# Constant products ahead of TensorE's long waits, the modulation sums over four layers, a reordered Fourier mixer

## The reference, cut to what matters

```
x = x + 0.5 * swiglu(rms_norm(x) ...)          # twice per layer, four times in block 1
u = rms_norm(x) @ w_in; x = x + concat(ssd(u), mlstm(u), rwkv7(u)) @ w_out
...
m = split(silu(c) @ ada_w[l] + ada_b[l])       # block 2, both for c and for c_ctx
h = rmsnorm(t) * (1 + m[scale]) + m[shift]
t = t + 0.5 * m[gate] * swiglu_2(h)            # before and after the mixer
layer 0: t = t + m[5] * (FFT2(h).real @ four_w + four_b)   # Fourier mixer
layer 1: retention mixer with rotary embedding, then a projection
return rmsnorm(x)
```

## Time and profile before

| | us |
|---|---|
| median of 3 executions | 3462.03 |
| lowest, highest | 3461.65, 3463.73 |
| the profiled execution's own time | 3463.73 |
| its span, first to last instruction | 3461.7 |
| PE busy in the span | 3247.6 (94%) |
| mean granted TensorE clock over the span | 0.972 |
| DVE, ACT, POOL busy | 2101.1 (61%), 1308.7 (38%), 115.8 (3%) |

### The profile page before, as it was taken

How to read it: one execution, slowest core, us unless ns; L and a number is a source line. 1 busy time by engine, 2 the same in 40 slices (tenths; PEclk the granted TensorE clock), 3 DMA queues, 4 the chain that set the end, 5 groups by cost and what they waited for, 6 DMA issues and landing times.

```text
span 3461.7 us, 45970 instructions
## 1 busy us (share of the span) xinstructions
PE 3247.6 (94%) x19010; PEld 2824.2 (82%) x19010; DVE 2101.1 (61%) x2545; ACT 1308.7 (38%) x1584; POOL 115.8 (3%) x126
## 2 busy tenths in 40 slices
PE   7998988999998898899999999999999999999998
PEld 7978877898988786798788877788878888787797
DVE  6757557776866657677775754775343333544654
ACT  4434244444435234543421233422233122444443
POOL 0001200000000210000000000000000000000000
PEclk9999999999999998999999999999999999999999
DMA  6542022555553112455443531343222222323452
GB/s 250 230 152 86 27 95 77 200 235 204 211 207 104 38 60 72 177 208 211 153 164 123 183 124 37 122 165 122 91 85 98 91 98 80 118 98 109 164 183 98
DMA packets 83835, 462.96 MB, mean 134 GB/s; under 512 B 7573, under 2 KB 11285, under 8 KB 43562
## 3 DMA queue, kind: packets, MB, share of 16 engines
q1 hardware_dynamic: 77952, 451.45, 35.6%
q10 hardware_dynamic: 5674, 8.57, 0.8%
HBM read 458.95 MB, written 1.05 MB: 133 GB/s over the span
## 4 chain that ended last, share of the span: by engine, by line
PE 64%; DVE 25%; ACT 7%; issue 2%; DMA 0%; ACTq 0%; POOL 0%; DVEq 0%; POOLq 0%
PE ps L100 64%; DVE lo L311 8%; DVE acc L459 5%; ACT hi L305 3%; PE ps L546 1%; DVE acc L456 0%; DVE m0restMs L1980 0%; DVEq L86 0%; DVE xt L701 0%; DVE f11rot L875 0%; DVE f10rot L875 0%; DVE f20rot L875 0%; ACT f20hf_h L853 0%; ACT f11hf_h L853 0%; ACT f10hf_h L853 0%
## 5 line engine op out<-in xcount | busy, mean ns | idle before, releaser
L311 DVE TENSOR_TENSOR lo<-raw,hi 128x2048 fp32r<-128x2048 f32 (+1 forms) x357 | 809.6, 2268 | 622.8 <-ACT hi L305 601.5
L305 ACT ACTIVATE hi<-raw 128x2048 fp32r<-128x2048 f32 (+1 forms) x357 | 676.1, 1894 | 572.7 <-PE ps L100 541.9
L459 DVE SCALAR_TENSOR_TENSOR acc<-raw,sil,acc 128x512 f32<-128x512 f32 x504 | 379.0, 752 | 20.7 <-DVE f21hf_l L877 0.5
L100 PE MATMUL ps<-half00hs,hi 128*128 128x512 f32 x672 | 209.3, 393 | 0.6 <-DVE lo L311 0.6
L100 PE MATMUL ps<-half02hs,hi 128*128 128x512 f32 x672 | 209.0, 392 | 0.7 <-DVE lo L311 0.7
L100 PE MATMUL ps<-half10hs,hi 128*128 128x512 f32 x672 | 208.7, 392 | 0.8 <-DVE lo L311 0.7
L100 PEld LDWEIGHTS ps<-half10hs,hi 128*128 128x128 f32 x672 | 125.7, 188 | 28.5 <-DVE lo L311 1.6
L100 PEld LDWEIGHTS ps<-half02hs,hi 128*128 128x128 f32 x672 | 125.4, 188 | 27.6 <-DVE lo L311 1.1
L100 PEld LDWEIGHTS ps<-half00hs,hi 128*128 128x128 f32 x672 | 125.2, 188 | 27.3 <-DVE lo L311 1.0
L100 PE MATMUL ps<-half10hs,lo 128*128 128x512 f32 x352 | 137.6, 391 | 0.0
L100 PE MATMUL ps<-half02hs,lo 128*128 128x512 f32 x352 | 137.6, 391 | 0.0
(11 more groups left out here) (919 smaller groups left out, 7900.3 us busy)
## 6 DMA issues: line engine op xcount, KB each, us to landing
raw<-in_ffn_w_gate_up SPq DMA_DIRECT2D x88, 1024.0 KB, 9.0
raw<-in_ffn_gu SPq DMA_DIRECT2D x88, 1024.0 KB, 5.0
raw<-in_ffn_w_down SPq DMA_DIRECT2D x85, 1024.0 KB, 5.2
raw<-in_ada_w SPq DMA_DIRECT2D x72, 1024.0 KB, 5.1
raw<-in_w_in_t SPq DMA_DIRECT2D x28, 1024.0 KB, 5.0
raw<-in_ret_w_in SPq DMA_DIRECT2D x24, 1024.0 KB, 4.9
raw<-in_w_out SPq DMA_DIRECT2D x16, 1024.0 KB, 5.0
raw<-in_w_in_n SPq DMA_DIRECT2D x12, 1024.0 KB, 5.0
```

Source lines behind the costliest of these rows:

```text
L100: return p().matmul(o, l, r, start=start, stop=stop, skip_group_check=True)
L305: a().activation(self.high(w), self.raw[self.place(r)][:, 0:width], ACT.Copy).then_inc(*a.mark(self.wac, w))
L311: v().tensor_tensor(self.low(w), self.raw[self.place(r)][:, 0:width], self.high(w).bitcast(F32), ALU.subtract).then_inc(*v.mark(self.wdv, w))
L459: v().scalar_tensor_tensor(out=acc[:, n, :], in0=w[:, k, :], scalar=s, in1=acc[:, n, :], op0=ALU.mult, op1=ALU.add).then_inc(*v.mark(self. ...
```

## The change

It adds `Core.idle`, which issues n float32 products of 256 columns, the block of ones times two constant masks, into a PSUM bank that nothing else uses just then. No one reads the result. It is called in PE's queue ahead of these waits:

| place | bank, n |
|---|---|
| Norm, before the wait for the last `xs`: f11; f20, f21 | 0, 9; 4, 9 |
| the same for mn0, mn1 | 0, 8 |
| the same for half00; half02; half10, ret, half12 | 0, 23; 0, 13; 0, 15 |
| ProjRw before tile 2; Prep before `sq`; Rest before tile 3 | 2, 8; 7, 4; 7, 4 |
| Inv after `bv`, both rounds; Scan before `Yn` | 1, 11; 0, 11 |
| Ssd before `en`; at n = 0 (after a wait for `xt` 3); before `yn` (after a wait for `across` 0) | 4, 4; 0, 13; 1, 8 |
| Ret, last head; Out, first product | 0, 6; 0, 11 |

It drops `soon`: all four FFNs of block 1 take a fill in 2 of 3 gate/up phases, and now one for down groups 0, 2, 4, 6 and 8. It also moves steps in Fourier: the split of the small weight `wx` (one ACT, one DVE operation) goes from the end of sequence 0's second transform to a point ahead of it; two phases of the gates move in front of it as well; and the products with four_w wait for the parts they read, tile by tile, and no longer for the last part of all.

```diff
@@ line 295 of the kernel before @@
+    def idle(self, p, bank, n):
+        for _ in range(n):
+            mm(p, self.ps[bank][:, 0:256], self.ones, self.msk[:, 0:2, :].rearrange("p a b -> p (a b)"))
@@ line 504 of the kernel before @@
+    idle = None
@@ line 535 of the kernel before @@
         K.ada.clear(p)
+        if self.idle:
+            if len(self.rows) == 4 and not self.turn[0]:
+                self.before[0].row(p, 0, 1)
+            K.idle(p, *self.idle)
@@ line 1040 of the kernel before @@
                 p.wait_ge(*self.dv["us", 2 * q - 7])
+            if q == 2:
+                self.K.idle(p, 2, 8)
@@ line 1108 of the kernel before @@
         yield
+        K.idle(p, 7, 4)
@@ line 1313 of the kernel before @@
             x.then_inc(*p.mark(E, "bv", T))
+            K.idle(p, 1, 11)
@@ line 1500 of the kernel before @@
         Yc = M.Yc.rearrange("p (t h) n -> p t (h n)", t=2)
+        K.idle(p, 0, 11)
@@ line 1618 of the kernel before @@
         for q in range(7):
+            if q == 3:
+                K.idle(p, 7, 4)
@@ line 1803 of the kernel before @@
             if n == 3:
+                K.idle(p, 4, 4)
@@ line 1824 of the kernel before @@
         for n in range(10):
+            if n == 0:
+                p.wait_ge(*A["xt", 3])
+                K.idle(p, 0, 13)
@@ line 1838 of the kernel before @@
         yield
+        p.wait_ge(*D["across", 0])
+        K.idle(p, 1, 8)
@@ line 2386 of the kernel before @@
                 j = 2 * n + chunk
+                if j == 0:
+                    K.idle(p, 0, 11)
@@ line 2512 of the kernel before @@
                     yield
-        p.wait_ge(*self.dv["lo", 1, 4])
-        self.finish.gates.done(p)
                 j, c = 2 * q + jj, slice(t * 128, (t + 1) * 128)
+                p.wait_ge(*self.dv["lo", 1, q])
+                if at < 4 and q == 0:
+                    for n in ((), (37, 38), (39, 40), (41,))[t]:
+                        p.wait_ge(*self.dv["e", n])
+                    if t == 3:
+                        self.finish.gates.done(p)
                     if j == 7:
+                        p.wait_ge(*self.dv["lo", 1, 4])
@@ line 2566 of the kernel before @@
                     if g == 4:
-                        if s == 0:
-                            a.wait_ge(*self.second.all)
-                            a().activation(self.wxs[0][0:5, :], self.wx[0:5, :], ACT.Copy).then_inc(*a.mark(A, "wx"))
                     self.squares(a, 1)
+                elif (s, i) == (0, 15):
+                    a.wait_ge(*self.second.all)
+                    a().activation(self.wxs[0][0:5, :], self.wx[0:5, :], ACT.Copy).then_inc(*a.mark(A, "wx"))
@@ line 2628 of the kernel before @@
                         self.low(v, s, 3)
-                        if s == 0:
-                            v.wait_ge(*self.ac["wx"])
-                            v().tensor_tensor(self.wxs[1][0:5, :], self.wx[0:5, :], self.wxs[0][0:5, :].bitcast(F32),
-                                              ALU.subtract).then_inc(*v.mark(D, "wx"))
@@ line 2640 of the kernel before @@
                     self.norm_dve(v, 1)
+                    v.wait_ge(*self.ac["wx"])
+                    v().tensor_tensor(self.wxs[1][0:5, :], self.wx[0:5, :], self.wxs[0][0:5, :].bitcast(F32),
+                                      ALU.subtract).then_inc(*v.mark(D, "wx"))
@@ line 2779 of the kernel before @@
                 self.project(p, h + 1, 1)
+            if h == 3:
+                K.idle(p, 0, 6)
@@ line 2918 of the kernel before @@
-    def ffn(s, gates=(), soon=False, late=0):
+    def ffn(s, gates=(), late=0):
@@ line 2926 of the kernel before @@
                     fill(2)
-                elif j % (4 if soon else 3) < (3 if soon else 2):
+                elif j % 3 < 2:
@@ line 2934 of the kernel before @@
                         run(s)
-                    if s.nt == 2 and g[0] % 3 == 0:
+                    if s.nt == 2 and g[0] % 2 == 0:
@@ line 2962 of the kernel before @@
         s.since = since
+        norm.idle = None if before is setup else (0, 9) if which == 1 else (4, 9)
@@ line 2976 of the kernel before @@
                                   K.at(ROWS + 8192, f"mn{l}no", 3, 512), lambda c, s: K.col(l, "nm", c)))
+        norm.idle = 0, 8
@@ line 3077 of the kernel before @@
                                  (ROWS, 50176), 16384, [2, 3, 0, 1])
-    ffn(s, [norm, norm], soon=True, late=8)
+    norm.idle = 0, 23
+    ffn(s, [norm, norm], late=8)
@@ line 3085 of the kernel before @@
     four = put("four", Fourier(K, "four", half, 0, both, Gated(gates, both, rot)))
-    for s in (half, half, four, half, half, four, four, gates, four, four, gates, four, gates, four, gates, four, gates):
+    for s in (half, half, four, half, half, four, gates, four, gates, four, four, four, gates, four, gates, four, gates):
                                  90112)
+    norm.idle = 0, 13
                                  (45056, 67584), 69632)
+    norm.idle = 0, 15
```

## The result

| kernel | median us | lowest to highest | runs |
|---|---|---|---|
| before | 3461.77 | 3457.30 to 3469.38 | 8 |
| after | 3471.75 | 3467.02 to 3474.85 | 8 |

The ratio is 1.0026, with an interval of 1.0015 to 1.0037. That is 10 us slower, outside the range of 3420 to 3457, and of the other sign than forecast. The profiled execution took 3474.85 us, its span is 3472.9. Here is the page of after: the engines' busy time, the chain of waits, and the group of constant products.

What follows compares the result with a forecast made beforehand. PE bounds the kernel, busy 3247.6 of 3461.7 us, through its idle and slow-clock time. Terms -7.5+0+4.0+2.9+1.8+0.9+2.2+9.1+5.3 made 18.7 us faster than the profiled 3463.7, so 3445.0, or 3443 for the median; range 3420 to 3457.

Steps and rivals of the forecast that it cites:

- The price of a product: One float32 constant product of 256 columns on PE: 0.43 us at full clock, twice that at half.
- Overrun hidden: Rival, at the filled waits: products run faster than priced or slack behind takes the overrun; 3424 us, chance 0.20.
- Norms: Products ahead of norms: four row groups and half12 7.5 us slower; two row groups 0 (2 slower to 2 faster).
- fall put off: Rival, ten norms: clock falls during or behind full-clock transposes, hitting the first products; 8.5 us slower, 3452, chance 0.19.
- ProjRw: Products before tile 2, both layers: outlast waits by 0.3 and 0.4 us, 3.0 + 1.8 returns; 4.0 faster.
- Inv, Scan, Ssd, Out: Products in these stages: Inv 2.9, Scan 1.8, Ssd 0.9, retention's end and Out 2.2 us faster.
- clock is worth nothing there: Batches of 4 ahead of `en`, in Prep and in Rest: 1.6 us inside waits of about 2, effect 0.
- Modulation sums: FFN fills: f21 with f11's pattern 11.9 us faster, new down fills 2.8 slower; sum 9.1 faster (4 to 12).
- column sums only change places: PE's modulation sums: f10, f20 and f11 take six phases more, half02 six fewer, at no cost.
- Fourier: Reordered Fourier steps: first wait's cut 2.2 us, `fx` wait gone 2.1, dip 1.0; sum 5.3 faster (3 to 7).
- The slower case: Rival, all filled waits: overruns paid, clock falls just the same, all 24.7 us regained goes; 3468, chance 0.06.
- a wait filled with products has no pause left in it: Argument, at filled waits, against the rival that the clock falls just the same; no size of its own.

Runs made afterwards that it cites:

- The stretch with 9 products above: half02's transposes with 9 products ahead; kernel before plus fitted products (none in Rest and Ssd), f21's sparser gate fills and Fourier edit: 3448.28 us, ratio 0.9953.
- fitted counts: Kernel before with products at all the change's places, no batch longer than its wait by 0.43 us a product: 3456.20 us, ratio 0.9986.
- The fastest kernel here: Kernel before plus fitted products (none in Rest and Ssd), Fourier edit, f21's sparser gate and denser down fills: 3442.15 us, ratio 0.9939.

## Why the prediction was wrong, by its own steps

By parts: the products were to gain 4.3 us and cost 13.7, 18.0 off; 2.1 of that is the norms, 15.9 all other places, 4.7 of these Out's second batch. The schedule edits were to gain 14.4 and gave 5.1, 9.3 off. Nearly every sign that the prediction named as right came in (`acc`, f21, the clock nearly, the starts of the norms' transposes, ProjRw, the Fourier waits). They looked at the places that the change touches, and most of the loss came between these.

**The price of a product** was right: 300 products, and 23 of them take 10.09 us, 0.43 each and the tail. "Overrun hidden" is out: nothing takes it.

**Norms.** Right in sign and near in size: 9.6 slower for 7.5. The transposes started 9.9 us after PE's last product in half00 and 6.5 in half10 (9.7 and 6.3 forecast), and half02's rows of after show the form:

```profile
2166.64 7.57 PE L100 MATMUL ps<-msk 128*128 128x256 f32 x26
2174.04 2.13 PE L557 MATMUL ps<-msk,half02xs 128*128 128x128 f32 x18
2176.73 0.44 PE L557 MATMUL ps<-msk,half02xs 128*128 128x128 f32 x2 [0.56 <-ACT half02no L582]
...
2181.21 1.20 PE L100 MATMUL ps<-half02hs,half02hi 128*128 128x512 f32 x2
```

(the batch here takes longer than 13 x 0.43: the clock is 0.78 from PE's last product to the first transpose). After 18 fast transposes PE waits for ACT and DVE at each pair, and the whole takes 7.17 us for 7.54. The first product takes 1.20 for two, at half clock. So "fall put off" held here, with its mechanism as written, in half00, half02, half10 and the retention, the norms with four row groups. In the six others the clock is 1.00 over the transposes and the 3.4 us behind. With norm products alone half00 and half02 have no fall either, and that run is 9.6 slower all the same. So what the norms lost is overrun: in after the transposes start 2.8, 3.4, 1.5, 1.5 and 1.8 us later behind PE's last product than before (half00, half02, half10, retention, half12), for 9.0 forecast in all.

The Trainium skill, "TensorE: Matmul & The Clock Gate", Part 4 (PE-mode transpose) says that transposes don't count as busy in the same way. The fall in the rows above agrees with this, as it came during transposes at full clock. The stretch with 9 products above does not, with all 32 transposes at 1.00 and no fall, and neither does the end of the slow stretch in the earlier trace rows.

**ProjRw.** Right at the place: 34.75 and 34.84 us at full clock, for 34 to 35 forecast. The stretches of after:

```profile
248.20:282.95 34.75, 34.75 (x281) 34.06 (x280) 18.67 (x21) 16.44 (x20) 0.00 (x0) 1.00 0.28 100
1068.21:1103.05 34.84, 34.84 (x282) 34.12 (x280) 17.82 (x20) 15.74 (x19) 0.00 (x0) 1.00 0.31 105
```

**Inv, Scan, Ssd, Out: the step that failed most.** It was forecast that what PE regains behind a filled wait stays regained, 7.8 us net. The gains are there: the stretches behind Inv's waits take 8.8 for 10.5 us in both layers, those behind Scan's 10.0 for 11.7. What failed is that other stretches would keep their clock. In layer 0 the main part of Scan went from 53.0 to 56.6 us in the run with products only, of which 0.8 is overrun. Of the kernel before and of that run:

```profile
448.61:501.62 53.01, 47.89 (x339) 38.93 (x339) 29.69 (x39) 27.05 (x35) 4.01 (x4) 0.94 0.34 115
```
```profile
448.37:504.95 56.58, 55.32 (x360) 45.33 (x361) 29.69 (x39) 27.04 (x35) 4.01 (x4) 0.89 0.32 108
```

Clock 0.89 for 0.94 is 12.4 us slow for 6.4. One trace could be chance, but the others agree. In the six traced kernels without products in Inv and Scan this stretch takes 51.9 to 53.3 us over both layers (mean 52.8), with 4 to 7 us slow. In the three with the change's counts it takes 53.8 to 56.6 (mean 55.6), with 6 to 12.5 slow. Less 0.8 of overrun that is 2.0 us a layer, over half of the 3.4 a layer that came back behind Inv's two waits; with fitted counts, which have no overrun, the mean is 53.6. Taken together mix0 and mix1 were to be 9.6 us shorter; they are 3.2 longer in the mean of these three. Which of the mixers' batches moves a fall where was not run one by one. The fall is no property of the place. In the run with f21's fills in its down part, the mixers have the code and order of before, and yet this short stretch of layer 0 is slow in part in one and not in the other (before, then that run):

```profile
323.04:331.77 8.73, 7.58 (x60) 6.35 (x61) 5.38 (x11) 4.02 (x10) 1.89 (x2) 1.00 0.01 3
```
```profile
321.11:331.41 10.30, 9.15 (x60) 7.55 (x61) 5.39 (x11) 4.03 (x10) 1.89 (x2) 0.83 0.01 2
```

1.6 us come and go with nothing changed there. I had read each clock of the earlier trace rows as belonging to its stretch, and made differences between the twins into prices; part of them was this. What sets where a fall comes, beyond work and waits, these runs leave open. The rest of this step's loss is in two places. In Rest and Ssd the short batches were costed at 0 since "clock is worth nothing there", and the one for `yn` as a two-row norm, 0: true of the stretch itself, false of the one behind it. In Out 11 products were counted where 22 run, 4.7 us that could be read from the loop, and the first batch started 1.0 late.

**Modulation sums.** 9.1 faster forecast, about 2 measured as the difference of two medians (5.1 without products less 3.1 by Fourier), 4 by the stages. f21's own part was right: the waits for `acc` went, and from its first transpose to PE's last product it takes 207.9 us, for 205 to 208:

```profile
1448.46:1656.38 207.92, 201.39 (x1417) 188.46 (x1416) 161.83 (x179) 93.51 (x104) 1.65 (x3) 0.99 0.56 221
```

The failed part is "column sums only change places", at no price. 20 phases in each FFN and not 18 shift where the sums fall, since a sum comes after every second tile of the modulations' weights, which is every four phases. PE's sums alone in f20's down part, and in half00 and half02 (gate part, down part), of after:

```profile
772.67:840.37 67.70, 1.84 (x16) 1.00 0.65 257
1666.31:1810.81 144.50, 11.04 (x96) 0.99 0.42 148
1810.81:2064.99 254.18, 9.20 (x80) 0.99 0.39 137
2174.04:2319.01 144.97, 11.04 (x96) 0.99 0.42 145
2319.01:2570.11 251.10, 0.00 (x0) 0.99 0.28 97
```

and of before:

```profile
768.83:833.25 64.42, 0.14 (x2) 1.00 0.63 248
1666.44:1807.87 141.43, 9.20 (x80) 0.99 0.42 148
1807.87:2063.11 255.24, 11.04 (x96) 1.00 0.40 138
2172.92:2314.45 141.53, 9.20 (x80) 0.98 0.42 148
2314.45:2565.93 251.48, 3.68 (x32) 1.00 0.31 107
```

16 records are one sum, 1.8 us of PE. f20's down part got one and is 3.3 longer; its gate part is 1.3 shorter, which leaves 1.9. The gate parts of half00 and half02 got one each at their very end, and their down parts lost one and two. PE waits for the `mods` right behind, 1.39 and 1.46 us, where before it waited once:

```profile
1810.81 0.50 PE L100 MATMUL ps<-hi,half00hf 128*128 128x512 f32 x1 [1.39 <-DVE mods L474]
...
2319.01 0.50 PE L100 MATMUL ps<-hi,half02hf 128*128 128x512 f32 x1 [1.46 <-DVE mods L474]
```

Without products half02 is 1.3 longer, f20 1.9, f10 and f11 0.5 shorter; half00's 2.2 is no finding by itself. Where f21 alone was changed (with its denser down fills), half02 and f20 stayed within 0.1 us of before, and 6 to 8 us were gained.

**Fourier.** Mechanism right for the waits, size 3 for 5.3. The two waits gave 2.7 and 2.2 for 2.5 and 2.1. The sines cost 0.9 for 0.3, and the dip, which was to give back 1.0, costs 1.0 more.

**The rivals.** The slower case named the right sign and half of the reason: overruns paid, dips staying. That its 3468 lies near 3471.75 is in part luck, since the gains behind ProjRw's, Inv's and Scan's waits did come, and what ate them was not in its sum: Out's second batch, the `mods` sums, falls in other stretches. It had 0.06, because I held that "a wait filled with products has no pause left in it". The filled wait has none, but the transposes behind it have: in the wide norms PE waits at each pair.

## What to carry to other kernels

Fill a wait only where the work behind it is paced by PE, and never past the wait's end: batches of 0.43 us a product cost 13.7 us when too long (4.7 of it by a batch with no wait at all) and gained 5.0 when fitted. Ahead of transposes that DVE and ACT empty, full clock gained half a microsecond at a place and nothing in the median, and the slow stretch may be handed on to products that need the clock. Judge a filled wait by the whole stage, up to the next one, and not by the stretch right behind. Before pricing an inserted batch count how often its condition holds in the loop, and for work spread by counters follow the counter to the end of the program, as a shift of six phases moved sums in stages that the edit doesn't name.

## What the hardware showed that I had not expected

The mean clock rose by 0.011 and the time by 0.3%: 76 us less at 1.2 GHz bought no time. Much of it had lain over waits and over work that DVE and ACT pace, and batches that outlast their waits ate what came back. The fastest kernel here has clock 0.985, the slowest, with products only, 0.986. And the same instructions in the same order can be fast in one kernel's trace and slow in the next: 1.6 us over the 60 records above, 3.5 us over a mixer stage, in kernels whose programs are the same up to there. Whether that differs from kernel to kernel or from execution to execution one trace of each can't tell.
